# Hybrid recurrence with a mixture of experts: 16x16 blocks of each triangular inverse computed on GpSimd one tile ahead

## What is computed

```
def step(S, inp):
    r_t, w_t, k_t, v_t, kk_t, a_t = inp
    sa = jnp.einsum("bhvk,bhk->bhv", S, -kk_t)
    S = (S * w_t[:, :, None, :] + sa[..., None] * (kk_t * a_t)[:, :, None, :]
         + v_t[..., None] * k_t[:, :, None, :])
    return S, jnp.einsum("bhvk,bhk->bhv", S, r_t)
...
x = x + gt1 * (jnp.concatenate([y_r, y_g], axis=-1) @ lp["w_out"])
h = rmsnorm(x, lp["norm2_g"]) * (1 + sc2) + sh2
```

## Time and profile before

| what | value |
|---|---|
| median of 3 runs (lowest, highest) | 1555.64 us (1551.04, 1555.64) |
| the profiled execution | 1553.69 us, of it the span of the trace 1552.0 us |
| mean granted TensorE clock | 0.961 of full |
| PE busy | 1437.4 us (93%) |
| DVE busy | 522.6 us (34%) |
| ACT busy | 369.2 us (24%) |
| POOL busy | 197.8 us (13%) |
| the recurrence block, tiles 0 to 8 | from about 484 to about 1005 us |

### The profile page before, as it was taken

One profiled execution on the slowest core, in us unless ns is written; L12 is line 12 of the kernel. 1 busy time (PEld: TensorE's weight loads), 2 busy tenths in 40 slices (PEclk: granted clock), 3 DMA queues, 4 the chain that ended last, 5 costly groups with the idle time before them and its releaser, 6 DMA issues. The chain is left out here.

```text
span 1552.0 us, 28560 instructions
## 1 busy us (share of the span) xinstructions
PE 1437.4 (93%) x12027; PEld 1040.5 (67%) x12027; DVE 522.6 (34%) x986; ACT 369.2 (24%) x765; POOL 197.8 (13%) x323
## 2 busy tenths in 40 slices
PE   5899999999996999999999999966999999999965
PEld 3566666566664877777777786735877878788832
DVE  4245644720201444444444454345000010000027
ACT  5332232401202323223233332220011111111132
POOL 4002212200002202012012011011000000000043
PEclk9999999999997999999999999976999999999987
DMA  9337656622141371312412302027879997988457
GB/s 351 102 97 242 229 149 227 233 71 84 57 129 51 100 235 45 110 40 72 110 34 79 110 14 64 1 61 271 314 256 374 384 390 287 325 327 326 164 209 266
DMA packets 168473, 271.19 MB, mean 175 GB/s; under 512 B 18760, under 2 KB 89030, under 8 KB 168344
## 3 DMA queue, kind: packets, MB, share of 16 engines
q1 hardware_dynamic: 153480, 221.65, 42.6%
q0 software_dynamic: 12560, 39.29, 6.7%
q10 hardware_dynamic: 2304, 8.39, 1.3%
HBM read 214.70 MB, written 54.59 MB: 174 GB/s over the span
## 5 line engine op out<-in xcount | busy, mean ns | idle before, releaser
L2294 PEld LDWEIGHTS banks<-moe_xT,moe_wg 128*128 128x128 f32 x1024 | 131.3, 191 | 8.9 <-issue 7.8
L2294 PE MATMUL banks<-moe_xT,moe_wg 128*128 128x128 f32 (+4 forms) x1024 | 135.4, 291 | 0.8 <-DVE moe_xT L2617 0.8
L2294 PE MATMUL banks<-moe_xT,moe_wu 128*128 128x128 f32 (+4 forms) x1024 | 134.5, 290 | 0.5 <-DMA moe_wu<-w_expert_up 0.5
L2294 PEld LDWEIGHTS banks<-moe_xT,moe_wu 128*128 128x128 f32 x1024 | 131.2, 191 | 0.7 <-DMA moe_wu<-w_expert_up 0.7
L1653 POOL TENSOR_TENSOR mixer_LTm<-mixer_LT,level 128x256 f32<-128x256 f32 (+1 forms) x90 | 71.9, 822 | 405.3 <-ACT mixer_LTo L1721 281.2
L664 PE MATMUL banks<-xT,w_v 128*128 128x352 f32 (+1 forms) x384 | 118.6, 469 | 1.8 <-ACT sig_w L808 1.8
L664 PE MATMUL banks<-xT,w_r 128*128 128x352 f32 (+1 forms) x384 | 118.6, 469 | 0.0
L664 PE MATMUL banks<-xT,w_k 128*128 128x352 f32 (+1 forms) x384 | 118.3, 468 | 0.0
L1349 PE MATMUL banks<-mixer_w_out,mixer_yT 128*128 128x512 f32 x256 | 117.6, 617 | 0.0
L2323 PE MATMUL banks<-moe_wd,moe_hid 128*128 128x512 f32 x256 | 112.5, 593 | 0.0
L664 PEld LDWEIGHTS banks<-xT,w_v 128*128 128x128 f32 x384 | 72.8, 190 | 45.6 <-issue 2.8
(11 more groups left out here) (489 smaller groups left out, 1944.2 us busy)
## 6 DMA issues: line engine op xcount, KB each, us to landing
moe_wg<-w_expert_gate SPq DMA_DIRECT2D x16, 2048.0 KB, 9.0
moe_wu<-w_expert_up SPq DMA_DIRECT2D x16, 2048.0 KB, 12.7
...
```

Source lines behind the costliest of these rows:

```text
L2294: mm = pe.matmul(bank[:, i * n:(i + 1) * n], wt[:, p % 2, q, (t0 + i) * P:(t0 + i + 1) * P], xT[:, p % 2, q, 0:n], start=q == 0, stop=q == ...
```

## The change

Levels 1 to 3 of the doubling, the 2 x 2 start and the swap are gone. In their place GpSimd computes the inverses of the 16 x 16 blocks on the diagonal by substitution: 64 blocks of a tile (8 heads, 8 blocks), one per partition, 256 elements each, in 30 dependent instructions (`substitution`: a mask, an addition of the identity, and 14 pairs of a multiplication and an addition, with a wait on itself after each). Levels 4 and 5 stay.

For tiles 2 to 8 the way of the numbers is: TensorE makes the scores of tile n + 1 in tile n (`diagonal_scores`, now behind gvar, in banks 0 and 1); ScalarE copies them to LT and issues two stores to a DRAM buffer; SyncE gathers the diagonal blocks into U16 in runs of 16 elements, GpSimd inverts, SyncE stores V16 and loads it again as `blocks` in the layout of the tile; VectorE spreads it over four column places with a mask (`spread`) and transposes it in squares of 32 x 32. TX holds TT and TI, now one pair for each parity of n. For tiles 0 and 1 the projection block makes the diagonal scores (8 groups of 4 matmuls in bank 7), ScalarE keeps them in LTd and issues four stores, and GpSimd inverts both tiles at once, on 128 partitions, between two of its feature stores.

The order of a tile is written anew. w_out comes in its four pieces between MT, RBT, RKT and ATT, with its first half in bank 4 and its second in bank 2. U stands between X6 and Y6. Of the sums, var now comes ahead of gvar. SyncE loads rows 0 to 20 and 28 to 36 of the features when O and Y are done, and the gates (20 to 28, 36 to 40) when yg and yr are done, in `load_gates`. In tile 0 the transposes and scores come ahead of its levels.

```diff
+def diagonals(d, u):
+    return d["scores"][u].rearrange("m (b e) -> (m b) e", b=4)[:, 0:1024].rearrange("b (r c) -> b r c", c=64)[:, :, 0:16]
...
+def substitution(pool, U, N, V, part, strict, ident, m, then, last):
+    G_ = pool
+    then(G_.tensor_tensor(N[0:m], U[0:m], strict[0:m], ALU.mult))
+    then(G_.tensor_tensor(V[0:m], N[0:m], ident[0:m], ALU.add))
+    for r in range(14, 0, -1):
+        shape = [m, r, 15 - r]
+        to = part[0:m, 0:r * (15 - r)].rearrange("p (s t) -> p s t", s=r)
+        rows = V[0:m, 0:r, r + 1:16]
+        then(G_.tensor_tensor(to, N[0:m, 0:r, r:r + 1].to_broadcast(shape), V[0:m, r:r + 1, r + 1:16].to_broadcast(shape), ALU.mult))
+        add = G_.tensor_tensor(rows, rows, to, ALU.add)
+        (last if r == 1 else then)(add)
...
+            pool.wait_ge(sg("first_scores_out"), 64)
+            for u in range(2):
+                pool.dma_start(U16[64 * u:64 * u + 64, :, :], diagonals(d, u)).then_inc(sg("first_U16_loaded"), 16)
             store("R", F_QD, out["R"], NJ + 1)
...
+            pool.wait_ge(sg("first_U16_loaded"), 32)
+            substitution(nc.gpsimd, U16, N16, V16, part16, c["strict16"], c["ident16"], P, then, then)
+            for u in range(2):
+                pool.dma_start(d["inverse"][u], V16[64 * u:64 * u + 64, :, :].rearrange("p s t -> p (s t)")).then_inc(sg("first_V16_out"), 16)
...
+            def diagonal(j, g):
...
+                for u in range(2):
+                    for v in range(2):
+                        at = slice(P * u + 64 * v, P * u + 64 * v + 64)
+                        mm = pe.matmul(banks[64 * v:64 * v + 64, 7 * 512 + 64 * (2 * u + g):7 * 512 + 64 * (2 * u + g) + 64],
+                                       out["B"][q, at], out["A"][q, at], start=True, stop=True)
+                mm.then_inc(sg("diagonal_done"), 1)
...
+            def keep_diagonal(j):
+                act.wait_ge(sg("diagonal_done"), 2 * j + 2)
+                nc.scalar.copy(LTd[:, :, :, j, :], banks[:, 7 * 512:7 * 512 + 256].rearrange("p (u g c) -> p u g c", u=2, g=2)).then_inc(sg("diagonal_read"), 1)
...
-            def load_feats(n, u, m):
-                before = reg(sp, n - 1)
-                for name in ("O_done", "Y_done", "yg_made", "yr_made"):
-                    w(sp, name, before)
...
+            def load_feats(n, m):
+                u, cols = n % 2, bass.ds(n * P, m)
+                w(sp, "O_done", n - 1)
+                w(sp, "Y_done", n - 1)
+                for lo, hi in ((0, 20), (28, 36)):
                     sp.dma_start(feats[u][:, lo:hi, 0:m], feat[:, lo:hi, cols]).then_inc(sg(f"feats{u}_loaded"), 16)
...
+                u, cols = n % 2, bass.ds(n * P, m)
+                w(sp, "yg_made", n - 1)
+                w(sp, "yr_made", n - 1)
+                for lo, hi in ((20, 28), (36, 40)):
...
+            def load_diagonals(n):
+                w(sp, "scores_out", 32 * (n - 1) if n < NP else 32 * (NP - 2) + 16)
+                w(sp, "V16_made", n - 2)
+                sp.dma_start(U16[:, :, :], diagonals(d, n % 2)).then_inc(sg("U16_loaded"), 16)
...
+            def store_inverse(n):
+                w(sp, "V16_made", n - 1)
+                w(sp, f"blocks{n % 2}_loaded", 16 * (n // 2))
+                sp.dma_start(d["inverse"][n % 2], V16[:, :, :].rearrange("p s t -> p (s t)")).then_inc(sg("V16_out"), 16)
...
+            def load_blocks(n, m):
+                w(sp, "V16_out", 16 * (n - 1))
+                w(sp, "TX_made", 2 * (n - 1))
+                of_tile = d["inverse"][n % 2].rearrange("(j b) (r c) -> (b r) j c", b=8, c=16)
+                sp.dma_start(blocks[0:m, n % 2], of_tile[0:m]).then_inc(sg(f"blocks{n % 2}_loaded"), 16)
...
+            for n in range(2, NT):
+                m = P if n < NP else DEC
+                load_feats(n, m)
+                load_diagonals(n)
+                load_gates(n, m)
+                if n == 2:
+                    later_loads()
+                store_inverse(n)
+                load_blocks(n, m)
...
+                                w(pe, f"TI{1 - half}_made", 2 * n + 2)
...
-                            mm = pe.matmul(psum[(4 if late else 6) + half][0:m, :], yT[:, q, 0:m], w_out[:, q, 512 * half:512 * half + 512],
...
+            def diagonal_scores(n, m):
...
+                scores(psum[0:2], F[:, F_B:F_B + NJ, :], F[:, F_A:F_A + NJ, :], m, "LT")
...
-                fill = {(1, 1): ["TB", "mu"], (2, 0): ["TV", "TGV"], (2, 1): ["gvar", "TK"], (3, 0): ["TKI", "var"], (3, 1): ["MT"], (4, 0): ["RBT"],
-                        (4, 1): ["RKT"], (5, 0): ["ATT"], (5, 1): ["wo0a", "wo0b", "wo1a", "wo1b"]}
...
+                if n == 0:
+                    for turned in (tb, tv, tgv, tk, tki, mt, rbt, rkt, att):
+                        turned()
+                    for g in range(2):
+                        product(0, 4, g, P)
+                    level(4)
...
+                else:
+                    tb()
+                    behind("mu")
+                    level(4)
+                    tv()
+                    tgv()
+                    for g in range(2):
+                        product(n, 5, g, m)
+                    behind("var")
+                    tk()
+                    level(5)
+                    tki()
+                    behind("gvar")
+                    if m_next:
+                        diagonal_scores(n + 1, m_next)
+                    mt()
+                    if not last:
+                        behind("wo0a")
+                    rbt()
+                    if not last:
+                        behind("wo1a")
+                    rkt()
+                    if not last:
+                        behind("wo0b")
+                    att()
+                    if not last:
+                        behind("wo1b")
...
+            def invert(n):
...
+                w(pool, "U16_loaded", 16 * (n - 1))
+                w(pool, "V16_out", 16 * (n - 2))
...
+                substitution(nc.gpsimd, U16, N16, V16, part16, c["strict16"], c["ident16"], 64, then, last)
...
+            for n in range(NT):
+                m = P if n < NP else DEC
+                masks(n, m)
+                if n > 1:
+                    invert(n)
...
+            def lt(n, m):
...
+                if n > 1:
+                    w(act, "U16_loaded", 16 * (n - 3))
+                    for g in range(2):
+                        w(act, f"LT{g}_read", 3 * n + m // 64)
+                    for h in range(m // 64):
+                        act.dma_start(scores_of_half(d, n % 2, h), LT[64 * h:64 * h + 64].rearrange("p g i c -> p (g i) c")).then_inc(sg("scores_out"), 16)
+                if m == P:
+                    for g in range(2):
+                        nc.scalar.copy(LTo[:, n % 2, g, :, :], psum[g][0:64, :].rearrange("p (a b) -> p a b", a=4)[:, :, 64:P]).then_inc(sg(f"LT{g}_read"), 1)
...
+                def spread(n, m):
+                    w(dve, f"blocks{n % 2}_loaded", 16 * (n // 2 + 1))
+                    for g in range(2):
+                        w(dve, f"TTx{g}_made", 3 * (n - 1))
+                    base = TX[0:m, n % 2, 0].rearrange("p g i (b c) -> p (g i) b c", b=4)
+                    V.tensor_tensor(base, blocks[0:m, n % 2].unsqueeze(2).to_broadcast([m, 8, 4, 16]),
+                                    c["quarter"][0:m, :].unsqueeze(1).unsqueeze(3).to_broadcast([m, 8, 4, 16]), ALU.mult).then_inc(sg("TX_made"), 1)
+                    w(dve, "TX_made", 2 * n + 1)
+                    V.transpose(TX[0:m, n % 2, 1].rearrange("p g i c -> p (g i c)"), TX[0:m, n % 2, 0].rearrange("p g i c -> p (g i c)")).then_inc(sg("TX_made"), 1)
...
+                else:
+                    mu()
+                    update(4)
+                    scaled_states()
+                    yr()
+                    update(5)
+                    pair_of_masks("MT", MT, "after", "G_done")
+                    yg()
+                    pair_of_masks("RBT", RBT, "upto", "Y_done")
+                    pair_of_masks("RKT", RKT, "upto", "Y_done")
+                    attention()
```

519 lines of the change are left out of this document (267 added, 252 removed).

## The result

The changed kernel takes **1483.74 us**, the median of 4 runs (1480.93 to 1485.87), against 1555.64 before. The ratio is 0.9539, with a 95% interval of 0.951 to 0.9568. The profiled execution took 1484.75, of it a span of 1482.9. The forecast was 1478, with its own case from 1467 to 1486.

The account below looks back on a forecast made before the run. TensorE's work was taken to bound the tiles, with GpSimd's chain hidden. Terms of -72, -3.2, -4.5, +2.2 and +0.9 sum to -76.6 us, giving a forecast of 1478 us, range 1467 to 1507.

Parts of the forecast that it names:

- its own case: Whole run: the forecast of 1478 us holds, within 1467 to 1486; chance 0.52.
- The pitch of a tile: Full recurrence tiles: 58.62 us less 11.0 of removed work and waits plus 0.7 of new waits, 48.3.
- Tiles 1 to 7: Recurrence: seven tiles at 10.3 us less each, 72 us saved; some 6 us of stalls left as they are.
- The GpSimd chain: Recurrence tiles: inversion takes 14.0 us, blocks there at 38.7, wanted at 41.3, so hidden; rival that it is late 0.17.
- The decision point: Recurrence tiles: GpSimd's chain becomes the new bound from 16.6 us for the inversion, 0.46 per small instruction.
- The port: Rival, recurrence tiles: GpSimd delays two VectorE passes on the h2 wait, 1.0 us per tile, 1485; chance 0.10.
- Projection block: Projection block: eight added groups of four matmuls at 0.27 us each cost 2.2; everything else there stays covered.
- Tile 0: First recurrence tile: 3 us saved up to the G rows, 1.6 behind, 1.5 taken off for low clock: -3.2.
- Tile 8 and the rest: Last tile up to G saves 4.5 us; behind it yg waits behind yr, +0.9; later blocks untouched.
- Exposed waits: Rival, recurrence tiles: waits counted as hidden (mu, spread, scores, load) show, 1 to 3 us per tile, 1494; chance 0.17.
- a sign of being wrong at once: Steady recurrence tiles: a granted clock below 1.0 would show the prediction wrong at once.
- The rivals on the chain: Recurrence: GpSimd's chain bounds, 1510 or 1540 (chance 0.17), or makes the run slower than before, about 1572 (0.03).

Follow-up runs that it names:

- the other profile: The changed kernel run once more, unaltered, against the kernel before: 1483.79 us, ratio 0.9546; tile 0 took 52.5 us.

## Why the prediction came out as it did

**The pitch of a tile: right, 0.4 short.** Forecast 48.3, measured 48.74. The levels and the swap are gone as counted, and the waits are those named: h2 0.38 (said 0.3), mu 0.18 (said 0.4), none before the scores, none before the first product. The largest mis-sized term is w_out: four pieces standing alone take 3.63 each, 14.5, where 16 matmuls in a row took 13.94. I moved them at no cost, and it is 0.6.

**Tiles 1 to 7: -70.2 against -72, in part by luck.** Seven quiet pitches give -69.2. Beyond its quiet pitch the kernel before spent 8.4 us in these tiles and the changed one 7.3. I had left such stalls as they are; in fact the largest of before went (4.8 us in tile 1 became 0.4) and three stretches at 1.2 GHz came, 1.55 us each. That the two nearly cancel was not foreseen.

**The GpSimd chain: right, with compensating parts.** Said: gather landed at t = 19.6, inversion 14.0, blocks there at 38.7, wanted at 41.3. With t = 0 at 603.87 the trace has 20.8, 11.8, 37.3 and 41.7. The row of a 16 element instruction at 0.31 was too dear: 14 elements take 0.21 and 56 take 0.29, with 0.08 between two. The lower bound of 0.20 fixed was nearer. The longer gather and the shorter inversion offset each other in part. The decision point was put at 16.6 us for the inversion; the kernel with 32 more instructions puts it at 16.3. Spread and transpose, for which there was no row, take 0.69 and 0.71, as taken.

**The port: right that it is hidden, wrong about who waits.** The rival had VectorE's passes on the h2 wait delayed. In the trace GpSimd's instruction at 632.12 takes 0.61 instead of 0.29 beside VectorE's add of two SBUF operands (631.85 to 632.59), so it ended 0.14 after the add: GpSimd waited. VectorE's add took 0.74 against 0.69 undisturbed, and over all tiles of this profile such adds take 0.69 to 0.81. TensorE's wait for h2 is 0.38 in each of the tiles 3 to 7 (0.54 in tile 2), whatever the adds took. For GpSimd's wait the trace agrees with the Trainium skill, SBUF — State Buffer, section SBUF: two separate sides: an exclusive lock, for whole instructions, to whichever came first. For VectorE's it agrees less well: the add started 0.19 before GpSimd's instruction of 631.75 ended and lost only 0.05.

**Projection block: mis-sized.** I priced a group of four matmuls by dividing a product of 16: 0.27. It takes 0.45, 3.6 in all. That this is nearly the +3.7 measured is chance: TensorE ended the block 4.9 us later and then waited 1.1 less for its features, and over all profiles of kernels with the change the first scores start between 496.9 and 501.1.

**Tile 0: wrong.** The step that failed is the last of its sum: "I take off 1.5 because the clock there is 0.61 of full ... and new waits can keep it there: -3.2". The direction of the correction was right and its size was not. I counted five turns through bank 6 and three masks as waits, by their length; I took the clock they leave behind at 1.5 us ahead of the G rows and at nothing behind them. Tile 0 missed the forecast by 8.4 us in this profile and by 3.2 in the other. Up to the G rows it took 36.8 us where the sum gives 34.9, and behind them 20.1 where it gives 13.7 (36.0 and 15.7 in the other profile). So 6.4 of the 8.4 lie behind G, where there is no new wait, only the low clock that followed X6's. The kernel before had long waits at the start of tile 0 alone, and its clock was back at 2.4 GHz from 505 on, with the score groups woven into the levels:

```profile
498.54 1.23 PE L1420 MATMUL banks<-mixer_M,swap 128*128 128x128 f32 x4 [2.38 <-DVE mixer_M L1907]
502.29 1.97 PE L1317 MATMUL banks<-mixer_TI,mixer_LTm 64*64 64x64 f32 x32 [2.52 <-issue]
...
505.62 0.65 PE L1317 MATMUL banks<-mixer_XX,mixer_TT 64*64 64x64 f32 x16
```

The changed one went in and out of 1.2 GHz until 551. With X6's wait of 2.0 taken away tile 0 was 11.0 us shorter than in the one profile and 5.7 than in the other.

**Tile 8 and the rest: right within 1 and 3 us.** -5.4 against -4.5, and -2.5 against +0.9. At the end of the recurrence the clock was at 2.4 GHz for more of w_out: from G of tile 8 to the transposes of h2 pass 40.5 us instead of 42.0. But at the first matmul of the experts only 0.4 of this is left (57.0 against 57.4). The other 2 us came in later blocks, which the change doesn't touch; why is open.

**Exposed waits** of 1 to 3 us per tile, the rival with 0.17, did not come. The stretches of 1.2 GHz that came in every second tile, 1.55 us each, were in no case of mine, though the kernel before has one like them (60.2 instead of 58.6 for the tile at 846). I had named a clock below 1.0 in steady tiles as a sign of being wrong at once. It came (0.97), and cost 4.7 us in all: the sign was too strict.

**Slips in the working.** The scores' features are there at t = 8.5 by the terms given, not 8.7. The sum of -76.6 on the median of 1555.64 gives 1479.0, not 1478. The rivals on the chain count 8 tiles, but only seven inversions are chained in the recurrence, and in the kernel with 32 more instructions six tiles waited. None of this changes what the prediction said would bound a tile.
